# Bringing an expert's rows back to the tokens: one fp32 product against two fp32r products, with the rows split into a high and a low part

## The reference

```python
def moe_swiglu(h, w_router, w1, w3, w2):
    logits = jnp.einsum('bsd,de->bse', h, w_router).astype(jnp.float32)
    top_val, top_idx = lax.top_k(logits, TOP_K)              # TOP_K = 2
    top_w = jax.nn.softmax(top_val, axis=-1)
    gates = jnp.sum(jax.nn.one_hot(top_idx, N_EXPERTS, dtype=jnp.float32) * top_w[..., None], axis=-2)
    out = jnp.zeros_like(h)
    for e in range(N_EXPERTS):                               # 8 experts, hidden width 3584
        out = out + gates[..., e:e + 1].astype(h.dtype) * swiglu(h, w1[e], w3[e], w2[e])
    return out
```

## Time and profile before

| | |
|---|---|
| Time, three runs | 1433.6, 1433.8 and 1432.38 us, median 1433.6 us |
| The profiled execution | 1433.79 us, of which the span from its first to its last instruction 1432.0 us |
| TensorE (PE) busy | 1394.3 us, 97% of the span |
| VectorE (DVE) busy | 340.7 us, 24% |
| ScalarE (ACT) busy | 277.9 us, 19% |
| Experts on TensorE | 0.50 ms to 1.42 ms of the span, one expert every 114.8 us |
| Mean granted TensorE clock | 0.987 of full |

### The profile page before, as it was taken

One profiled execution on the slowest core, in us unless ns is written; L12 is line 12 of the kernel. 1 busy time (PEld: TensorE's weight loads), 2 busy tenths in 40 slices (PEclk: granted clock), 3 DMA queues, 4 the chain that ended last, 5 costly groups with the idle time before them and its releaser, 6 DMA issues.

```text
span 1432.0 us, 32932 instructions
## 1 busy us (share of the span) xinstructions
PE 1394.3 (97%) x14890; PEld 816.7 (57%) x14890; DVE 340.7 (24%) x420; ACT 277.9 (19%) x353; POOL 21.1 (1%) x36
## 2 busy tenths in 40 slices
PE   6999899999999999999999999999999999999996
PEld 4998788888998833534543443453453353454343
DVE  4568555435566510010010001001001001000001
ACT  4454443323652300000000000001001000000001
POOL 1000000000000000000000000000000000000000
PEclk9999999999999999999999999999999999999998
DMA  6833555513736499999999999999999999999960
GB/s 229 301 119 137 206 197 196 191 59 119 273 119 233 165 366 387 392 377 382 402 375 379 405 385 365 393 400 365 392 396 373 385 397 374 383 397 378 376 252 32
DMA packets 140354, 431.36 MB, mean 301 GB/s; under 512 B 12346, under 2 KB 18778, under 8 KB 140096
## 3 DMA queue, kind: packets, MB, share of 16 engines
q1 hardware_dynamic: 138672, 424.01, 78.3%
q0 software_dynamic: 1552, 5.32, 1.1%
HBM read 427.19 MB, written 2.10 MB: 300 GB/s over the span
## 4 chain that ended last, share of the span: by engine, by line
PE 95%; DVE 2%; DMA 1%; ACT 1%; issue 1%; SPq 0%; POOL 0%; DVEq 0%; POOLq 0%; ACTq 0%
PE psum L1636 41%; PE psum L1663 20%; PE psum L1222 8%; PE psum L1224 8%; PE psum L1223 8%; PE psum L1646 2%; PE psum L1677 2%; PE psum L1394 1%; DMA raw<-in_w_mix_in 1%; DVE wlo L804 0%; DVE h L817 0%; PE psum L1609 0%; PE psum L1241 0%; PE psum L1610 0%; ACT whi L564 0%
## 5 line engine op out<-in xcount | busy, mean ns | idle before, releaser
L1636 PE MATMUL psum<-ring,xe 128*32 128x512 f32 (+1 forms) x5952 | 568.9, 538 | 0.0
L1636 PEld LDWEIGHTS psum<-ring,xe 128*32 128x32 f32 x5952 | 189.5, 110 | 345.0 <-issue 310.9
L1663 PE MATMUL psum<-ring,gT 128*32 128x256 f32 x5376 | 296.0, 379 | 0.6 <-ACT gT L737 0.6
L1663 PEld LDWEIGHTS psum<-ring,gT 128*32 128x32 f32 x5376 | 174.6, 110 | 125.8 <-issue 13.8
L1119 DVE TENSOR_TENSOR gate<-gate,psum 128x768 f32<-128x768 f32 (+1 forms) x32 | 27.3, 855 | 601.2 <-ACT gate L732 601.2
L804 DVE TENSOR_TENSOR wlo<-raw,whi 128x2048 fp32r<-128x2048 f32 (+1 forms) x67 | 147.4, 2229 | 52.4 <-ACT whi L564 52.3
L564 ACT CAST whi<-raw 128x2048 fp32r<-128x2048 f32 (+1 forms) x67 | 122.3, 1860 | 58.3 <-PE psum L1224 32.5
L1222 PE MATMUL psum<-whi,f_hi 128*128 128x512 f32 (+1 forms) x320 | 126.1, 394 | 5.8 <-DVE wlo L804 5.0
L1224 PE MATMUL psum<-whi,f_lo 128*128 128x512 f32 (+1 forms) x320 | 123.2, 385 | 0.0
L1223 PE MATMUL psum<-wlo,f_hi 128*128 128x512 f32 (+1 forms) x320 | 123.1, 385 | 0.0
L737 ACT COPY gT<-psum 128x768 f32<-128x768 f32 (+1 forms) x32 | 23.0, 720 | 453.7 <-PE psum L1646 453.7
(11 more groups left out here) (207 smaller groups left out, 837.6 us busy)
## 6 DMA issues: line engine op xcount, KB each, us to landing
ring<-in_moe_w SPq DMA_DIRECT2D x672, 512.0 KB, 5.9
raw<-in_ffn_w SPq DMA_DIRECT2D x33, 1024.0 KB, 6.1
raw<-in_w_mix_in SPq DMA_DIRECT2D x22, 1024.0 KB, 7.1
raw<-in_w_mix_out SPq DMA_DIRECT2D x8, 1024.0 KB, 5.0
raw<-in_w_mix_in SPq DMA_DIRECT2D x4, 544.0 KB, 5.4
x<-in_x SPq DMA_DIRECT2D x2, 512.0 KB, 5.1
bias_by_distance<-setup_bias POOLq DMA_DIRECT2D x1, 1024.0 KB, 5.1
bias<-bias_by_distance POOLq DMA_DIRECT2D x2, 512.0 KB, 7.4
```

The lines of the kernel that those rows point to most:

```text
L1636: ins = mm(banks(j)[o:o + 32, g, 0:2 * q].rearrange("p (i c) -> p i c", i=2), rows_[:, k * CAP + 32 * g:k * CAP + 32 * (g + 1)], w[:, kk, ...
L1663: ins = mm(bank[6 + g // 2][32 * q:32 * (q + 1), 256 * (g % 2):256 * (g % 2 + 1)], gT[:, a:a + 32], w[:, o:o + 256], start=j == 0 and n == ...
```

## The change

`y` becomes two fp32r tiles. ScalarE's copy out of PSUM now casts to `y_hi`; VectorE then computes `y_lo` = PSUM minus `y_hi` with the helper `rest` and signals a new semaphore, `y_split`, for which TensorE waits instead of `y_sb`. `pickT` is written as fp32r (it holds 0 and 1 only). `scatter` issues for each `t` and `g` four products with `y_hi` and then four with `y_lo`, into the same PSUM columns. `y_lo` lies where `h` lies, which is not in use between the gather and the final norm.

```diff
-        y = place("y", GROUPS * 256)
-        pickT = place("pickT", GROUPS * SEQ)
+        y_hi = place("y_hi", GROUPS * 256, F32R)
+        y_lo = place("y_lo", GROUPS * 256, F32R, offset=h_at)
+        pickT = place("pickT", GROUPS * SEQ, F32R)
...
-                nc.scalar.copy(y[:], psum[:, 6 * 512:6 * 512 + GROUPS * 256]).then_inc(y_sb, 1)
+                nc.scalar.copy(y_hi[:], psum[:, 6 * 512:6 * 512 + GROUPS * 256]).then_inc(y_sb, 1)
...
                     nc.vector.tensor_copy(xe[:], xe_all[:, ds(n * turn + n * (e + 1), n)]).then_inc(xe_sb, 1)
+                rest(y_lo[:], psum[:, 6 * 512:6 * 512 + GROUPS * 256], y_hi[:], y_sb, v + 1, y_split)
                 dve.wait_ge(back_ps, v + 1)
...
-                pe.wait_ge(y_sb, v + 1)
+                pe.wait_ge(y_split, v + 1)
                 pe.wait_ge(pickT_sb, v + 1)
                 for t in range(NT):
                     for g in range(GROUPS):
-                        for q in range(4):
-                            a = SEQ * g + t * P
-                            ins = mm(bank[3 + q][:, 256 * t:256 * (t + 1)], pickT[32 * q:32 * (q + 1), a:a + P],
-                                     y[32 * q:32 * (q + 1), 256 * g:256 * (g + 1)], start=g == 0, stop=g == GROUPS - 1)
+                        for part in (y_hi, y_lo):
+                            for q in range(4):
+                                a = SEQ * g + t * P
+                                ins = mm(bank[3 + q][:, 256 * t:256 * (t + 1)], pickT[32 * q:32 * (q + 1), a:a + P],
+                                         part[32 * q:32 * (q + 1), 256 * g:256 * (g + 1)],
+                                         start=g == 0 and part is y_hi, stop=g == GROUPS - 1 and part is y_lo)
                 ins.then_inc(back_ps, 1)
```

More of the change, by code:

```diff
@@ L303, in trunk @@
         diag_sb, rows_ps, rows_sb = sem("diag_sb"), sem("rows_ps"), sem("rows_sb")
-        y_sb, back_ps, added = (sem(n) for n in ("y_sb", "back_ps", "added"))
+        y_sb, y_split, back_ps, added = (sem(n) for n in ("y_sb", "y_split", "back_ps", "added"))
         rel_set = sem("rel_set")
```

## The result

| | before | after |
|---|---|---|
| Runs of this comparison | 1433.6, 1433.8, 1432.38, 1432.33 us | 1422.79, 1421.89, 1423.82, 1424.01 us |
| Median | 1432.99 us | 1423.3 us |
| Profiled execution / its span | 1433.79 / 1432.0 us | 1422.79 / 1421.0 us |
| Mean granted TensorE clock | 0.987 | 0.990 |

The ratio of after to before is 0.9931, 95% interval [0.9914, 0.9948]: the changed kernel is faster, by 9.7 us between the medians. The forecast was 8.2 us less, 1425.4 us, in a range from 1423.8 to 1429.5 us.

The account below looks back on a forecast made before the run. TensorE, busy in 97% of the span, was taken as the bound, so scatter time saved comes off the end. 7 x 1.15 + 0.15 = 8.2 us off the 1433.6 us median gave 1425.4 us, range 1423.8 to 1429.5.

Parts of the forecast that it names:

- The step of the scatter: Four records on TensorE in each expert's scatter: 0.120 us instead of 0.216, saving 1.15 us a scatter over 12 steps.
- rows 5: Profile rows where full-array fp32r products of 256 columns, weight load included, come every 0.12 us.
- rows 6: Profile rows where products of just 8 columns still come every 0.11 us, the time of a 128-column weight load.
- The subtraction: VectorE, once an expert: 1.0 us from cast to TensorE's release, covered in seven experts, paid in the last.
- a last scatter at the lower clock: Last expert's scatter at 1.2 GHz after its longer wait: at most another 1.66 us, held within the range's high end.
- TensorE's next waits and the weights: After the shorter scatter: VectorE's addition is not newly late, and the weight DMAs at 390 GB/s hide none of the gain.
- the ring's slack: Weight blocks land well before use: 25 us of slack against a whole gain of 8 us, even with DMAs no faster.
- The sum: Whole kernel: 7 x 1.15 us for seven experts plus 0.15 us for the last, 8.2 us less.
- Adding up over the row groups: Rival on the scatter: fp32r's 0.012 us overhead adds up over four row groups, step 0.156 us, 1428.8 us; chance 0.12.
- no gain in the step: Rival on the scatter: four PSUM banks take results no faster, step stays 0.216 us, 1434.6 us; chance 0.10.
- issue as the bound: Rival on the scatter: 48 products issued at 0.11 us each take 5.27 us, kernel slower at 1454.3 us; chance 0.10.
- the term for the runs' spread: Range's low end: 0.6 us taken off 1424.4 us for the spread of runs lying within 1.4 us, giving 1423.8.

## Why the prediction was right and where it was wrong

**The step of the scatter** was forecast at 0.120 us from rows 5 and measured at 0.118. An expert's period is 1.18 us shorter, not 1.15. The choice between the ends, "rows 5 differ from the new products only in the number of rows", was right, and so was the floor of 0.110 us from rows 6, which the narrow products show as 0.112. The 1.62 us of the scatter were forecast as 1.66.

**The subtraction** costs 0.96 us plus handovers, 0.99 us in the last expert (1.91 against 0.92 us of waiting), nothing in the other seven. That is shown by the run with the subtraction alone, whose periods did not change. The prediction also named a last scatter at the lower clock, "at most another 1.66 us"; it gave it no chance of its own, and it came in two of seven profiles, for 1.4 us in the fp32 scatter and 0.2 us in the fp32r one.

**TensorE's next waits and the weights**: no waits on either. TensorE has none between two scatters, SyncE's queue still waits for TensorE (142 times, 244.2 us, for the up products' blocks on the first of its two lines), and the DMAs moved 388 GB/s where 390 was worked out. The argument that the ring's slack exceeds the whole gain was not put to the test, since the DMAs simply went faster.

**The sum** was 8.2 us. By the spans from the first up product on it is 934.0 - 925.5 = 8.5 us. The 0.3 us are twelve steps of 0.002 us in eight scatters (0.2 us), and roundings.

**The rivals.** Adding up over the row groups (step 0.156 us), no gain in the step (0.216) and issue as the bound (0.11 us a product) are all refuted by the steps of 0.118 us. The run with narrow products puts the price of issuing a product with its load at 0.028 us or less, as a scatter of 48 sees it. The Trainium skill's page "TensorE: Matmul & The Clock Gate" gives, in the section "What happens when you issue a matmul", about 62 ns a matmul when hardware decode is off; an estimate from this figure made 2.98 us of the scatter, and it took 1.62. Whether that mode is off or decoding was far enough ahead stays open.

**What failed** is a size and not the mechanism: the term for the runs' spread in the low end of the range, "0.6 for the runs' own spread (they lie within 1.4 us)", and with it the median of three runs, 1433.6 us, as the point to subtract from. The three runs were a sample from the upper end of a wide distribution. 49 executions of the kernel before lie from 1428.99 to 1434.44 us, their median at 1431.45; the twelve of the changed kernel from 1420.51 to 1424.01, median 1422.6. Before's first four had their median 1.5 us above its own, and after's four drew clocks of 0.989 to 0.990. So the measured difference was 9.7 us for a change of 8.5. The trace could have warned: TensorE's mean granted clock was 0.987 while the clock was 1.00 from 490 to 1390 us. Of the 18.6 us that this mean lacks over the span, 13.7 lay in four stretches ahead of the experts and the rest in the last 10 us, behind the last scatter. I had read the clock only where the change is. The forecast lay 2.1 us too high: 2.15 us by the point to subtract from (1433.6 against 1431.45), 0.3 by the sum, and 0.35 us the other way, as 1431.45 - 8.5 is 1422.95 and the four executions had their median at 1423.3. That the miss of the range is just 0.5 us is luck: the twelve executions have their median at 1422.6. Not knowing the median of before, 1431.45 us, I should have let the low end reach at least 2 us further down.

## What to carry to other kernels

Where an fp32 product stands on the path, ask what two fp32r products in its place do to the number of records and of weight loads: here both stayed the same, each record's time was nearly half as long, and the step ended only a little above 0.112 us, which a quarter of the columns could not get below. The split costs a subtraction, which is free where other products stand between and costs a full microsecond where none do; in one execution it was 2.4 us, as the clock fell under the fp32 scatter that followed. And before you state how far the runs can lie from a forecast, look at the granted clock over the whole span and not only in the stage that changes: three runs within 1.4 us said nothing of the 5.4 us over which 49 runs spread.

## What the runs showed of the hardware that was not expected

- Products on different row groups of the array pass one another: with the high and the low product of each group next to each other in the program, the trace has all four high ones within 0.03 us and then the low ones, and the scatter takes 1.63 us instead of 1.62.
- Four fp32r products on four row groups, writing four PSUM banks at once, go at the pace of one on the full array: 0.118 us against 0.12. The small overhead of an fp32r product over half an fp32 step (0.108 us) is shared and does not add up.
- After a wait of 1.91 us TensorE's clock may fall in the middle of the products that follow: 0.99 for the first 1.3 us, 0.50 for the next 3.0, in one profile; in the run with reordered products it fell over the last two steps of twelve (0.55 over the last 0.6 us). In five others with the same wait it did not fall before the scatter's end.
- The same program, the kernel before, began its experts at 495.4 us in one profile and at 497.8 to 498.0 in three, with a granted clock of 0.91 or 0.83 over the same 20 us. Over thirteen profiles the start lies between 493.3 and 498.0 us and is the later, the more clock is lost in the pauses ahead of it.
